# The first two weight panels in four pieces each, between the two halves of x, and half of x's transposes inside the first panel

## What is computed

```python
h = x                                        # 256 x 1024
hn = rmsnorm(h, mix_norm[0])                 # h * rsqrt(mean(h^2) + eps) * gain
h = h + mixer_ab(hn, ab_w_in[0], ...)        # first: hn @ ab_w_in, columns "fb" (2048..2559) for the decay gates
h = h + conv_glu_ffn(rmsnorm(h, ffn_norm[0]), ...)
...                                          # gate, a second mixer, a second block with memory attention
return rms_norm(x, final_norm_g)
```

## Time and profile before

| what | value |
|---|---|
| median of 3 runs (lowest, highest) | 1068.91 us (1068.8, 1070.66) |
| the profiled execution | 1069.89 us, of which the traced span is 1068.2 us |
| TensorE busy, its weight loads | 1001.1 us (94%), 914.8 us (86%) |
| VectorE, ScalarE, POOL busy | 706.6 us (66%), 573.9 us (54%), 135.9 us (13%) |
| transfers | 174.38 MB, mean 163 GB/s |
| granted TensorE clock, mean | 0.98 |

### The profile page before, as it was taken

One profiled execution on the slowest core, in us unless ns is written; L12 is line 12 of the kernel. 1 busy time (PEld: TensorE's weight loads), 2 busy tenths in 40 slices (PEclk: granted clock), 3 DMA queues, 4 the chain that ended last, 5 costly groups with the idle time before them and its releaser, 6 DMA issues.

```text
span 1068.2 us, 16427 instructions
## 1 busy us (share of the span) xinstructions
PE 1001.1 (94%) x6656; PEld 914.8 (86%) x6656; DVE 706.6 (66%) x1011; ACT 573.9 (54%) x806; POOL 135.9 (13%) x124
## 2 busy tenths in 40 slices
PE   6998898999999989588999999989999989999996
PEld 6986778999988877468999988878988879999995
DVE  5887766788864656846888884565655557755664
ACT  6745636656643555655666553476555555434432
POOL 4012501243310000000233320001000000000000
PEclk9999999999999999799999999999999989999999
DMA  9552226687545445305666556644645433655541
GB/s 320 172 192 80 79 74 174 181 256 197 188 183 190 151 156 197 79 1 140 195 189 186 173 169 223 236 158 130 222 142 174 158 119 105 191 183 193 181 154 41
DMA packets 165643, 174.38 MB, mean 163 GB/s; under 512 B 4094, under 2 KB 132592, under 8 KB 165568
## 3 DMA queue, kind: packets, MB, share of 16 engines
q1 hardware_dynamic: 163376, 167.92, 50.2%
q0 software_dynamic: 2160, 5.41, 1.6%
q10 hardware_dynamic: 32, 0.01, 0.0%
HBM read 172.25 MB, written 1.07 MB: 162 GB/s over the span
## 4 chain that ended last, share of the span: by engine, by line
PE 74%; DVE 9%; ACT 9%; issue 5%; DMA 1%; POOL 1%; POOLq 0%; SPq 0%; ACTq 0%; DVEq 0%
PE bank L803 36%; PE bank L784 17%; PE bank L822 12%; PE bank L838 4%; ACT w_hi L1136 3%; DVE w_lo L1450 2%; PE bank L868 1%; DMA w_raw<-in_ab_w_in 1%; ACT le L1242 1%; DMA h<-in_x 1%; DVE le_s L1782 1%; DVE prod L1527 1%; POOL sp__80 L651 1%; ACT L1242 0%; ACT x_hi L1295 0%
## 5 line engine op out<-in xcount | busy, mean ns | idle before, releaser
L1450 DVE TENSOR_TENSOR w_lo<-w_raw,w_hi 128x2048 fp32r<-128x2048 f32 x157 | 358.7, 2289 | 192.2 <-ACT w_hi L1136 192.2
L1136 ACT ACTIVATE w_hi<-w_raw 128x2048 fp32r<-128x2048 f32 x157 | 299.9, 1915 | 278.1 <-PE bank L803 156.1
L803 PE MATMUL bank<-y_hi,w_hi 128*128 128x256 f32 x736 | 209.4, 285 | 4.0 <-issue 3.9
L803 PE MATMUL bank<-y_lo,w_hi 128*128 128x256 f32 x736 | 208.0, 283 | 0.0
L803 PE MATMUL bank<-y_hi,w_lo 128*128 128x256 f32 x736 | 207.0, 281 | 0.0
L803 PE MATMUL bank<-x_hi,w_hi 128*128 128x256 f32 x528 | 150.8, 286 | 0.7 <-DVE w_lo L1450 0.7
L803 PE MATMUL bank<-x_lo,w_hi 128*128 128x256 f32 x528 | 149.4, 283 | 0.0
L803 PE MATMUL bank<-x_hi,w_lo 128*128 128x256 f32 x528 | 149.4, 283 | 0.0
L803 PEld LDWEIGHTS bank<-y_hi,w_hi 128*128 128x128 f32 x736 | 139.1, 189 | 5.0 <-issue 4.5
L803 PEld LDWEIGHTS bank<-y_hi,w_lo 128*128 128x128 f32 x736 | 139.8, 190 | 0.0
L803 PEld LDWEIGHTS bank<-y_lo,w_hi 128*128 128x128 f32 x736 | 139.6, 190 | 0.0
(11 more groups left out here) (338 smaller groups left out, 1498.9 us busy)
## 6 DMA issues: line engine op xcount, KB each, us to landing
w_raw<-in_ffn_up SPq DMA_DIRECT2D x88, 512.0 KB, 5.2
w_raw<-in_w_in SPq DMA_DIRECT2D x35, 1024.0 KB, 5.3
w_raw<-in_ffn_down SPq DMA_DIRECT2D x22, 1024.0 KB, 5.0
w_raw<-in_ab_w_in SPq DMA_DIRECT2D x14, 1024.0 KB, 5.2
w_raw<-in_ple_gate SPq DMA_DIRECT2D x8, 1024.0 KB, 5.1
w_raw<-in_c_w_in SPq DMA_DIRECT2D x6, 1024.0 KB, 5.3
w_raw<-in_ab_w_out SPq DMA_DIRECT2D x4, 1024.0 KB, 5.1
w_raw<-in_c_w_out SPq DMA_DIRECT2D x4, 1024.0 KB, 5.1
```

The source lines that it names most:

```text
L803: mm = pe.matmul(bank[b][:, c * 256:c * 256 + 256], wv[w][:, k, c * P:(c + 1) * P], x[:, k, :], start=(k == 0 and m == 0 and not (first an ...
L1136: act.activation(whi[n % RING][:, :], raw[n % RAW][:, :], ACT.Copy).then_inc(*mark("weights_hi", ("hi", n)))
L1450: dve.tensor_tensor(wlo[n % RING][:, :], raw[n % RAW][:, :], plain(whi[n % RING][:, :]), ALU.subtract).then_inc(*mark("weights_lo", ("lo", ...
```

## The change

The loads of SyncE come in a new order: the identity, x's first half, pieces 0 and 1 of panel 0, x's second half, pieces 2 and 3 of panel 0, the four pieces of panel 1, then the whole panels from 2 on. A piece is a quarter of a panel (two row groups k, 512 columns of the raw buffer, 256 KB), and has its own transfer, its own w_hi and its own w_lo. The events ("hi", n) and ("lo", n) of a whole panel are those of its last piece. The list of steps now alternates turn j and piece j of panel 0, with the squares of a half as soon as its two turns are done; then come the stats, the pieces of panel 1 and split 2. On TensorE turns 2 and 3 move into panel 0 at k = 2; both panels run k outermost and wait for each piece's w_lo at every second k; the row of panel 1 is turned at k = 4 instead of k = 2.

```diff
@@ -29,6 +29,7 @@
 ROT = HEAD // 4
 LEVELS = [64, 32, 16, 8, 4, 2, 1, 0]
 RAW, RING = 3, 3
+PIECES, IN_PIECES = 4, (0, 1)
 BIAS_AT = 6
 MAGIC = float(0x5F3759DF)
 
@@ -242,11 +243,14 @@
 
         out.append(("split", first + 3 + RING))
 
-    out.extend([("split", 0), ("setup", 0)])
-    out.extend(("turn", "mix0", j) for j in range(4))
-    out.append(("split", 1))
-    out.extend(("square", "mix0", j) for j in range(2))
-    out.extend([("stats", "mix0"), ("split", 2)])
+    out.append(("setup", 0))
+    for j in range(4):
+        out.extend([("turn", "mix0", j), ("piece", 0, j)])
+        if j % 2:
+            out.append(("square", "mix0", j // 2))
+    out.append(("stats", "mix0"))
+    out.extend(("piece", 1, j) for j in range(PIECES))
+    out.append(("split", 2))
     gemm("fb")
     out.extend([("setup", 1), ("hg_decay",)])
     gemm("qb")
@@ -337,7 +341,7 @@
 
 
 
-TURN_INSIDE = {FIRST["wo0"] + 3: ("ffn0", 0, 1), FIRST["up0"]: ("ffn0", 2, 3), FIRST["kv"]: ("mix1", 2, 3),
+TURN_INSIDE = {FIRST["fb"]: ("mix0", 2, 3), FIRST["wo0"] + 3: ("ffn0", 0, 1), FIRST["up0"]: ("ffn0", 2, 3), FIRST["kv"]: ("mix1", 2, 3),
                FIRST["wo1"] + 3: ("ffn1", 0, 1), FIRST["up1"]: ("ffn1", 2, 3), FIRST["mk"]: ("mem", 2, 3)}
 INSIDE = {(k, j) for k, *js in TURN_INSIDE.values() for j in js}
 ROWS_AFTER = {FIRST["fb"]: "mix0", FIRST["up0"]: "ffn0", FIRST["up1"]: "ffn1", FIRST["mv"]: "blk2"}
@@ -591,6 +595,12 @@
                 sp.dma_start(dst, src).then_inc(*mark(f"load_{name}", ("loaded", name), by=16))
 
             load(ident[:, :], io["c_ident"], "ident")
+
+            def piece(n, j):
+                _stage, _i, name, _kind, (idx, where) = PANELS[n]
+                src = io[name][idx[0]][256 * j:256 * j + 256, where:where + 256].rearrange("(k p) n -> p k n", p=P)
+                dst = raw[n % RAW][:, 512 * j:512 * j + 512].rearrange("p (k n) -> p k n", k=2)
+                sp.dma_start(dst, src).then_inc(*mark(f"piece_loaded{n}{j}", ("raw", n, j), by=16))
 
             def panel(n):
                 stage, i, name, kind, (idx, where, *part) = PANELS[n]
@@ -618,12 +628,15 @@
                     src = w[:, where:where + 256].rearrange("(k p) n -> p k n", p=P)
                     sp.dma_start(raw[slot][:, :].rearrange("p (k n) -> p k n", k=KT), src).then_inc(*mark(f"panel_loaded{slot}", ("raw", n), by=16))
 
-            for n in range(len(PANELS)):
+            for half in range(2):
+                c = slice(512 * half, 512 * half + 512)
+                load(h[:, :, c], io["x"][0].rearrange("(t p) d -> p t d", p=P)[:, :, c], f"x{half}")
+                for j in (2 * half, 2 * half + 1):
+                    piece(0, j)
+            for j in range(PIECES):
+                piece(1, j)
+            for n in range(len(IN_PIECES), len(PANELS)):
                 panel(n)
-                if n == 0:
-                    for half in range(2):
-                        c = slice(512 * half, 512 * half + 512)
-                        load(h[:, :, c], io["x"][0].rearrange("(t p) d -> p t d", p=P)[:, :, c], f"x{half}")
                 if n == 3:
                     load(masks[:, :, :].rearrange("p a b -> p (a b)"), io["c_levels"], "levels")
                     load(reset[:, :], io["c_reset"], "reset")
@@ -755,7 +768,8 @@
                 stage, i, name, kind, where = PANELS[n]
                 xh, xl, k0, needs = XIN[stage]
                 wh, wl = whi[n % RING], wlo[n % RING]
-                pe.wait_ge(*at(("lo", n)))
+                if n not in IN_PIECES:
+                    pe.wait_ge(*at(("lo", n)))
 
                 def input_ready(k):
 
@@ -791,13 +805,15 @@
                     b = pb(n)
                     claim(b, ("ev", n))
                     wv = [w[:, :].rearrange("p (k n) -> p k n", k=KT) for w in (wh, wl)]
-                    first = i == 0
+                    first = i == 0 or n in IN_PIECES
                     for c, k in [(c, k) for k in range(KT) for c in range(2)] if first else [(c, k) for c in range(2) for k in range(KT)]:
                         if c == 0 and first:
                             if k == 2:
                                 turn_inside()
+                            if n in IN_PIECES and k % 2 == 0:
+                                pe.wait_ge(*at(("lo", n, k // 2)))
                             input_ready(k)
-                        if c == 0 and k == 2 and n - 1 in ROWS_AFTER:
+                        if c == 0 and k == (4 if n in IN_PIECES else 2) and n - 1 in ROWS_AFTER:
                             norm_row(ROWS_AFTER[n - 1])
                         for m, (x, w) in enumerate(((xh, 0), (xl, 0), (xh, 1))):
                             mm = pe.matmul(bank[b][:, c * 256:c * 256 + 256], wv[w][:, k, c * P:(c + 1) * P], x[:, k, :],
@@ -1135,6 +1151,12 @@
                         act.wait_ge(*at(("pe", n - RING)))
                     act.activation(whi[n % RING][:, :], raw[n % RAW][:, :], ACT.Copy).then_inc(*mark("weights_hi", ("hi", n)))
 
+            def piece(n, j):
+                act.wait_ge(*at(("raw", n, j)))
+                c = slice(512 * j, 512 * j + 512)
+                events = [("hi", n, j)] + ([("hi", n)] if j == PIECES - 1 else [])
+                act.activation(whi[n % RING][:, c], raw[n % RAW][:, c], ACT.Copy).then_inc(*mark("weights_hi", *events))
+
             act.dma_start(xn[0:2 * KT, 0, 0:P], io["mix_norm"].rearrange("l (a c) -> (l a) c", c=P)).then_inc(*mark("load_mix_gain", ("loaded", "mix_gain"), by=16))
 
 
@@ -1247,6 +1269,8 @@
                     panel(args[0])
                 elif kind == "split":
                     split(args[0])
+                elif kind == "piece":
+                    piece(*args)
                 elif kind == "setup":
                     if args[0] == 0:
                         act.wait_ge(*at(("tr", "gain0")))
@@ -1449,6 +1473,12 @@
                     dve.wait_ge(*at(("hi", n)))
                     dve.tensor_tensor(wlo[n % RING][:, :], raw[n % RAW][:, :], plain(whi[n % RING][:, :]), ALU.subtract).then_inc(*mark("weights_lo", ("lo", n)))
 
+            def piece(n, j):
+                c = slice(512 * j, 512 * j + 512)
+                events = [("lo", n, j)] + ([("lo", n)] if j == PIECES - 1 else [])
+                dve.wait_ge(*at(("hi", n, j)))
+                dve.tensor_tensor(wlo[n % RING][:, c], raw[n % RAW][:, c], plain(whi[n % RING][:, c]), ALU.subtract).then_inc(*mark("weights_lo", *events))
+
             def rest(src, gain, hi, lo, name, event, *first):
 
                 for before in first:
```

## The result

| | before | changed | ratio, 95% interval |
|---|---|---|---|
| median, us (13 runs each) | 1070.18 | 1073.59 | 1.0033 (1.0023 to 1.0043) |
| the profiled execution, us | 1069.89 | 1073.26 | |

The changed kernel is slower by about 3.5 us. That is above the range of the prediction, and on the other side of the bound that it had set for "no change". The median of the kernel before came out 1.3 us higher here than in the three runs shown ahead; by the ratio their time would become 1068.91 x 1.0033 = 1072.4, above the range too. A few executions of some kernels took 1426 to 3469 us and are left out of every ratio.

What follows compares the result with a forecast made beforehand. It took panel 4's transfer in a saturated queue, then ScalarE and VectorE, as the bound. TensorE's head start of 3.4 us shrank to 0 at panel 5; +0.4 on the chain gave 1069.3 by the median (1070.3 profiled), range 1067.2 to 1071.5.

Steps and rivals of the forecast that it cites:

- the bound that it had set for "no change": Whole kernel: times from 1066.8 to 1071.0 us, about 0.2% or 2.1 us, count as the same; chance 0.83.
- rival B: SyncE's wait before panel 3: panel 0's last w_lo after 14.6 us delays panel 4 one for one; 1070.6 to 1071.5, chance 0.17.
- The new opening, step by step: Opening to panel 0's end: x0 lands 5.0, first weight matmul 8.6, panel 0's last w_lo 15.0, TensorE ends panel 0 at 16.5.
- Who waits for the last w_lo of panel 0: SyncE issues panel 3 at about 15.05 instead of 10.80; panel 3 lands +0.45 us, panel 4 at 26.6, +0.4.
- The bound on the gain, 2.12 us by ScalarE's wait: ScalarE's wait for panel 4: even a much earlier landing brings at most 2.12 us through the chain.
- rival A: Opening transfers: x and the pieces run at 300 GB/s, panel 4 lands 1.6 us late; 1070.5, chance 0.10.
- the rule from the Trainium skill: Opening transfers: batch to at least 1 MiB for 75% of peak; 0.26 MB pieces would move slower, giving 1070.5.
- Rival E: TensorE's wait before panel 5 drops its clock to 1.2 GHz; hidden, else up to +1 us; chance uncovered 0.03.
- Theory K: From the follow-up runs: TensorE's clock later on, not the opening, makes the difference; the ratio stays near 1.003 with turns outside.
- The sum: Whole kernel: -3.4 us at first matmul, -1.5 at panel 0's end, 0 at panel 5, +0.4 on the chain; 1069.3.

Runs made afterwards that it cites:

- e4: The changed kernel with 15 unread transposes of the identity filling TensorE's idle stretches in the opening; ratio 1.0022 against the kernel before.
- e1: The changed kernel with turns 2 and 3 of x back ahead of panel 0 on TensorE; ratio 0.9999 against the kernel before.
- e5: The kernel before with the three tables of constants (1.11 MB) issued behind panel 6 instead of ahead of panel 4; ratio 0.9984.
- e6: The changed kernel with turns 2 and 3 ahead of panel 0 and the tables of constants behind panel 6; ratio 0.9976 against the kernel before.
- e11: The changed kernel itself, measured and profiled a second time; ratio 1.0038 against the kernel before.
- e10: The kernel before with x ahead of panel 0, panel 0 split whole between turns 1 and 2, tables behind panel 6, no pieces; ratio 1.0013.
- e12: e6 measured once more; ratio 0.9989 against the kernel before.

## Why the prediction was wrong

The reading of what the kernel waits for was right, and so was the way of the loss: the chain hangs on panel 4's transfer, the last w_lo of panel 0 comes late through the round trip over TensorE, SyncE is held, the queue has a gap near 15 to 18 us, and the loss passes on. That is rival B, priced as one of the lesser chances. It came out larger than B had it, 1073.59 against 1070.6 to 1071.5, and by another trigger than the two that B names (x0 at 6.5, half-speed pieces on ScalarE and VectorE). The step that failed is *The new opening, step by step*: its result, panel 0's last w_lo at 15.0, was 1.7 us too early (16.7). Its terms, measured against forecast:

- x0's landing 5.37 against 5.0: +0.37. From there to the first weight matmul at 9.14, forecast 8.6, 0.17 more.
- The 12 matmuls and turn 2: 3.76 us (9.14 to 12.90) against 2.6 (8.6 to 11.2): **+1.16**. I took the pace of 0.12 us from rows that stand behind 16 transposes without a gap. In the new opening TensorE does 8, waits 1.7 us and starts at about half that pace. e4 shows it: kept at work, the 12 take 1.68 us.
- From turn 2's result to the last w_lo: 3.8 against 3.8. The pieces' costs on ScalarE and VectorE (0.63 and 0.68 us busy, 0.52 and 0.61 between starts) were right.

The same pace undoes another line of that step. TensorE was to end panel 0 at 16.5, 1.5 us ahead, and to come to panel 5 at 40.0. It began panel 1 at 18.36 and came to panel 5 near 42.2. So it had nothing left to lose there, and that the wait came out at 2.5 us, against about 2.2 in the forecast, is luck.

Second, *Who waits for the last w_lo of panel 0*: panel 3's transit was right (5.0 against 4.9), but panel 4 landed 7.2 us behind panel 3, not the 6.2 to 6.7 that I had put down: after the gap the same bytes took longer, not shorter. I had argued that a gap would let the 16 engines come level; the three landings in e1, e4 and the changed kernel (6.9, 7.1, 7.2 us behind panel 3) speak against that. Why the bytes take longer is open. Together: 1.7 + 0.1 + 0.5 on top of +0.4 is 2.7, as measured. Rival B's point, "over 0.2% from panel 3's issue at 17.2", is what 4.9 and 6.2 give; with the measured 5.0 and 7.2 it lies at 16.1.

One count was off without harm: ten issues stand ahead of panel 2's instead of four, not three, and SyncE came to it at 7.22, not 5.6. The full queue hid that, as forecast.

The bound on the gain, 2.12 us by ScalarE's wait, held: e5 and e6, which remove that wait, gained 1.6 us. The small pieces did not move slower as a whole (the stream ran at 343 GB/s from 9 to 14 us, at 344 in the kernel before), so rival A and with it the rule from the Trainium skill, *DMA: Bandwidth & Descriptors*, section Bandwidth, had no part in the loss. Rival E happened in the way it was described and was covered: TensorE's granted clock fell to 0.50 from 46 to 48 us after its wait of 2.46 us, and VectorE still found panel 5's result in time.

Over and above the shift of the chain, 2.7 us, the medians differ by 0.7 us more. That part lies inside the interval. Theory K may have a share in it: the mean granted clock of an execution is 0.979 or less in 18 of the 24 of the changed kernel (with e11's), and in 25 of the 104 of the kernel before that ran beside e1, e5, e10 and e12. One stretch at the lower clock, that of rival E, is covered; what the others cost was not tested.

The chances were mis-set as well. The sum put panel 3's issue at 15.05, already past the point (14.6) from which it has every delay pass on one for one. An error to the late side counted in full, one to the early side for 0.45 us at most. With such a knee the loss side deserved the larger half. Nor is the knee sharp: e1 issued panel 3 at 14.47 and still had panel 4's split 0.8 us late.

## What to carry to other kernels

When a transfer is held by a buffer's release, cost a reordering at that release first. Here the whole change delayed the issue by 6 us. The full queue hid most of it; the last 2.3 us, from the work moved between two pieces of a split, emptied the queue, and the kernel paid 2.7 us, while TensorE, for which the change was meant, was not on the chain. Ask of each byte in a saturated opening when it is first needed: moving 1.11 MB of constants behind three more panels was worth more than all the piecing. A matmul pace read behind unbroken work need not hold behind a wait.

## What the hardware did that I had not expected

TensorE's pace in the opening: 0.213 us between 256-column matmuls (the 1.2 GHz level) from 9.14 to 14.6 us, and again from 14.61 to 18.4 in e10, both behind a wait (1.7 and 5.0 us). In e1 a wait of 1.15 us stands between the first 8 and the next 8 transposes, none ahead of the matmuls, and they too run at 0.213 from 10.49 to 13.5. In the kernel before, behind 16 unbroken transposes, and in e4, where the idle stretches are filled but for 1.2 and 0.6 us, it is 0.12 from nearly the first matmul on. The trace's first record of the clock starts where the pace changes in each: at 12.42 us in the kernel before, 9.72 in e4, 13.54 in e1, 14.58 in the changed kernel, 18.56 in e10.

The same program can differ by 3.7 us, mostly through the clock. The changed kernel's two profiles had the scan at 39.35 and 39.59, and executions of 1073.26 and 1069.57 us. Most of the difference arises in one stretch. First the profile of the changed kernel, then that of e11, the chain at 132 us:

```profile
131.99 1.19 PE bank L987 x2
133.18 0.43 PE bank L988 x2
133.61 0.43 PE bank L989 x2
```

```profile
132.17 0.67 PE bank L987 x2
132.84 0.22 PE bank L988 x2
133.06 0.22 PE bank L989 x2
```

In the first, TensorE ran at half pace behind its wait (granted clock 0.50 from 132 to 136 us), in the second at full pace, and the products that start at 144.29 in the one start at 141.83 in the other: 2.6 us. The waits differ too, 4.08 us in the first and 1.16 in the second. In the second TensorE had been at 0.50 from 126 to 130 us, with work that is not on the chain, and so was busy until 131; in the first it had done that work at full pace. Another 0.7 us arises between 407 and 503 us, where the first has one stretch at 0.50 more, from 438 to 441. Of the 13 runs of either kernel the times spread over 3 to 5 us. A single profile of this kernel therefore says little by its span; the place of a marked instruction ahead of such a stretch is the better measure, and it is what the table goes by.
